# A two-block network on one core: the odd layer's last value units between its heads, maxima broadcast by DMA, low parts in halves, and gates evicted with their functions

## The reference

```
first_block:  proj = rmsnorm(x) @ w_in                     # 3592 columns
              h += [fox_attention(8 heads), hgrn(4 heads)] @ w_out
              h += memory_cross_attention(rmsnorm(h), rmsnorm(mem), w_q, w_kv, w_o)
              h += relu(rmsnorm(h) @ w1)^2 @ w2
second_block: cond = silu(c)
  layer 0:    x += g1 * pool_attention_mixer(modulate(rms_norm(x)))
              x += g2 * ((silu(h @ w1) * (h @ w3)) @ w2),  h = modulate(rms_norm(x))
  layer 1:    x += g1 * mlstm_mixer(modulate(rms_norm(x)))
              x += g2 * (the same gated FFN)
hgrn:         f = lb + (1 - lb) * sigmoid(gf); g = log f; k = 1 - f; q = silu(gq); i = gi
              S_t = diag(f_t) S_{t-1} + k_t i_t^T;  o_t = S_t^T q_t;  rmsnorm(o) * silu(gg)
mlstm:        z = h @ w_in                # q|k 1024, v 1024, o 1024, gates 32
              q, k = silu(conv5(z_qk)); per head and direction, with F = cumsum(log f):
              w[s,t] = exp(F_t - F_s + i_s - m_t), masked to one side
              y_t = sum_s (q_t.k_s / 8) w[s,t] v_s / max(|sum_s ...|, exp(-m_t))
              out = sigmoid(o) * head_gain * rms_norm(y_forward + y_backward) @ w_out
```

## Time and profile before

| | us |
|---|---|
| median of three runs | 2356.7 (2354.33 to 2357.33) |
| the profiled execution | 2348.1 |
| its span | 2346.0 |
| PE busy | 2171.9 (93%) |
| POOL busy | 818.5 (35%) |
| mean granted clock of PE | 0.948 |

### The profile page before, as it was taken

One profiled execution on the slowest core, in us unless ns is written; L12 is line 12 of the kernel. 1 busy time (PEld: TensorE's weight loads), 2 busy tenths in 40 slices (PEclk: granted clock), 3 DMA queues, 4 the chain that ended last, 5 costly groups with the idle time before them and its releaser, 6 DMA issues.

```text
span 2346.0 us, 26426 instructions
## 1 busy us (share of the span) xinstructions
PE 2171.9 (93%) x10170; PEld 1730.2 (74%) x10170; DVE 1121.2 (48%) x1852; ACT 710.1 (30%) x970; POOL 818.5 (35%) x295
## 2 busy tenths in 40 slices
PE   6998978898899999989988999999999878999998
PEld 5885367786778878876357888887798557888887
DVE  4112594453388886554536666722375554111112
ACT  3124533333332232333433212223233323222221
POOL 2441042461334334434013443333343332444342
PEclk8997878999899999988999999999999889999999
DMA  4230002241445553321014555532231002332322
GB/s 136 88 101 1 1 10 74 95 138 36 157 148 179 179 179 108 103 90 54 1 49 149 180 180 179 167 98 77 90 100 63 1 17 73 99 99 90 107 85 77
DMA packets 220417, 226.14 MB, mean 96 GB/s; under 512 B 3787, under 2 KB 218524, under 8 KB 220188
## 3 DMA queue, kind: packets, MB, share of 16 engines
q1 hardware_dynamic: 220316, 224.78, 29.5%
HBM read 222.67 MB, written 2.10 MB: 96 GB/s over the span
## 4 chain that ended last, share of the span: by engine, by line
PE 80%; DVE 8%; issue 7%; ACT 3%; POOL 1%; DMA 0%; DVEq 0%; SPq 0%; ACTq 0%; POOLq 0%
PE ps L1690 23%; PE ps L1692 23%; PE ps L1691 23%; PE ps L1821 2%; PE ps L1801 1%; DVE adacc L1368 1%; PE ps L1906 1%; PE ps L1843 1%; PE ps L1794 1%; PE ps L1757 1%; ACT wH L631 1%; PE ps L1812 1%; DVE T L1064 1%; DVE uL L1049 1%; DVE hnL L1051 0%
## 5 line engine op out<-in xcount | busy, mean ns | idle before, releaser
L511 POOL TENSOR_TENSOR wL<-raw,wH 128x2048 fp32r<-128x2048 f32 (+2 forms) x161 | 729.4, 4531 | 1274.3 <-ACT wH L631 1259.4
L1690 PE MATMUL ps<-hnH,wH 128*128 128x512 f32 x1336 | 530.8, 397 | 26.1 <-DVE hnL L1051 14.4
L1692 PE MATMUL ps<-hnH,wL 128*128 128x512 f32 x1336 | 526.1, 394 | 0.0
L1691 PE MATMUL ps<-hnL,wH 128*128 128x512 f32 x1336 | 525.5, 393 | 0.0
L631 ACT ACTIVATE wH<-raw 128x2048 fp32r<-128x2048 f32 (+2 forms) x161 | 302.4, 1879 | 648.8 <-PE ps L1692 624.8
L1690 PE MATMUL ps<-uH,wH 128*128 128x512 f32 x864 | 341.6, 395 | 10.5 <-DVE uL L1049 8.2
L1692 PE MATMUL ps<-uH,wL 128*128 128x512 f32 x864 | 338.6, 392 | 0.0
L1691 PE MATMUL ps<-uL,wH 128*128 128x512 f32 x864 | 338.5, 392 | 0.0
L1690 PEld LDWEIGHTS ps<-hnH,wH 128*128 128x128 f32 x1336 | 254.6, 191 | 80.7 <-issue 28.9
L1692 PEld LDWEIGHTS ps<-hnH,wL 128*128 128x128 f32 x1336 | 253.9, 190 | 54.0
L1691 PEld LDWEIGHTS ps<-hnL,wH 128*128 128x128 f32 x1336 | 254.6, 191 | 52.4 <-issue 0.5
(11 more groups left out here) (327 smaller groups left out, 2452.4 us busy)
## 6 DMA issues: line engine op xcount, KB each, us to landing
raw<-in_ffn_w_dram SPq DMA_DIRECT2D x60, 1024.0 KB, 5.3
adaw<-in_ada_w_dram SPq DMA_DIRECT2D x48, 1024.0 KB, 7.3
raw<-in_w_dram SPq DMA_DIRECT2D x32, 1024.0 KB, 5.3
raw<-in_w_in_dram SPq DMA_DIRECT2D x14, 1024.0 KB, 5.4
raw<-in_od_w_in_dram SPq DMA_DIRECT2D x12, 1024.0 KB, 5.3
raw<-in_w_xkv_dram SPq DMA_DIRECT2D x8, 1024.0 KB, 5.3
raw<-in_ffn_w_dram SPq DMA_DIRECT2D x8, 768.0 KB, 4.2
raw<-in_ev_w_in_dram SPq DMA_DIRECT2D x5, 1024.0 KB, 5.2
```

The source lines that it names most:

```text
L511: nc.gpsimd.tensor_tensor(wL[n % 2][:, 0:kc, 0:c], raw[n % 2][:, 0:kc, 0:c], wH[n % 2][:, 0:kc, 0:c].bitcast(F32), ALU.subtract).then_inc( ...
L1690: nc.tensor.matmul(out_ap, wh, xh, start=first, stop=False)
L1691: nc.tensor.matmul(out_ap, wh, xl, start=False, stop=False)
L1692: return nc.tensor.matmul(out_ap, wl, xh, start=False, stop=last)
```

## The change

1. `low` is made in two halves over k, so `w_lo` counts two for a unit (and SP's wait is for both). `unit_ready` waits for the first half, and a new `unit_whole` for the second, at the middle of a feature unit's first block; token units wait for both at once.
2. The gates' six units of the first stage are evicted by ACT straight from the banks with Silu or Sigmoid. The forget row's chain on ACT moves from unit 8 to unit 11, the four Ln come at unit 12, and DVE's gate steps stand ahead of the fox attention.
3. `norm_highs` makes the second unit's high after its third chunk. 
4. In `out`, ACT's squares of x are spread between other work, and xkv's second high stands ahead of the last two of them.
5. In the odd layer the output-gate units come first (units 5 to 8), one value unit is left ahead of the heads (unit 9), and three (10 to 12) run between the heads, in 18 portions of 5, 5 and 6 chunk steps (a step is 3 matmuls), three portions per head in heads 0 to 5, in banks 4 and 5. Their highs are made by ACT at odd heads, their lows by POOL at the end of heads 1, 3 and 5; `od_out`'s unit 0 is the last of these, and the high of its unit 1 is made at head 7 (hence `gated_norm` from 1), with its low on POOL behind the last head. DVE takes a block at the fifth tile of heads 1 to 6. The convolutions stand beside the takes of q and k and of the output gates. SP writes the maxima once to DRAM and reads each of the 16 rows back, broadcast over 128 partitions, into a ring of four SBUF tiles; L2122 is gone. The weights lie in four slots of four tiles, and the decayed scores are written over them; `ma` is gone. ACT's exps of slot s wait for `l_o` of slot s-4.

```diff
@@ -91,7 +91,7 @@
             add("od_w_in_2", 0, KC, 3104 - P, P, 1)
-            for c0 in range(D, 3 * D, UC):
+            for c0 in (*range(2 * D, 3 * D, UC), *range(D, 2 * D, UC)):
                 add("od_w_in_2", 0, KC, c0, UC)
@@ -111,9 +111,23 @@
-BY_ACT = [u[0].startswith("ffn_w1") for u in UNITS for _ in range(u[5])]
+GATE_UNITS = (7, 8, 9, 10, 13, 14)
+BY_ACT = [u[0].startswith("ffn_w1") or n in GATE_UNITS for n, u in enumerate(UNITS) for _ in range(u[5])]
 TAKEN = [sum(not x for x in BY_ACT[:b]) for b in range(len(BY_ACT) + 1)]
...
+V_FILL = (BLOCK0[AT["od_in"][0] + 10], BLOCK0[AT["od_in"][0] + 13])
+def bank(b):
+    return 4 + b % 2 if V_FILL[0] <= b < V_FILL[1] else b % 4
+def last_in_bank(b):
+    return b - 2 if V_FILL[0] + 2 <= b < V_FILL[1] else b - 4
@@ -312,9 +331,15 @@
     hgain = place("hgain", [P, D], F32, AR + 49408)[0]
-    wt = [place(f"wt{i}", [P, S], F32, ULOFF + 2048 * i)[0] for i in range(WT_RING)]
+    wt = []
+    for i in range(4):
+        offset = [ULOFF + 5120 * i] * TB
+        for j in range(1, TB):
+            offset[j] = offset[j - 1] + 512 * (TB - j + 1 if i % 2 == 0 else j)
+        if i == 3:
+            offset = [AR + 57088, ULOFF + 15360, AR + 55552, AR + 53504]
+        wt.append([place(f"wt{i}{j}", [P, (TB - j if i % 2 == 0 else j + 1) * P], F32, offset[j])[0] for j in range(TB)])
     cy = place("cy", [P, KC, S], F32, UHOFF)[0]
-    ma = [[place(f"ma{i}{d}", [P, TB, S], F32, HN + 8192 * (2 * i + d))[0] for d in range(2)] for i in range(2)]
     hsq = T
@@ -494,7 +522,21 @@
             sp.dma_start(hgain[:], a["od_head_gain_2"].rearrange("o h v -> o (h v)").to_broadcast([P, D])).then_inc(gain_in, 16)
-            loads(AT["od_in"][0] + 2, AT["ff2_1"][0])
+            n = AT["od_in"][0]
+            loads(n + 2, n + 12)
+            sp.wait_ge(r_rows, 2)
+            sp.dma_start(mrows, Mrow[:]).then_inc(mrow_out, 16)
+            sp.wait_ge(mrow_out, 16)
+            sp.wait_ge(r_tr, 2)
+            for s in range(2 * ML_H):
+                h, d = s // 2, s % 2
+                if s >= BC_RING:
+                    sp.wait_ge(l_w, 4 * (s - BC_RING) + 4)
+                row = h + 32 * d
+                sp.dma_start(bcr[s % BC_RING][:], mrows[row:row + 1, :].to_broadcast([P, S])).then_inc(bc_in[s % BC_RING], 16)
+                if s in (3, 7, 11, 15):
+                    load(n + 12 + s // 4)
+            loads(n + 16, AT["ff2_1"][0])
             gated_ffn(1)
@@ -508,8 +550,9 @@
                 pool.wait_ge(w_hi, (n if value is None else value) + 1)
-                nc.gpsimd.tensor_tensor(wL[n % 2][:, 0:kc, 0:c], raw[n % 2][:, 0:kc, 0:c],
-                                        wH[n % 2][:, 0:kc, 0:c].bitcast(F32), ALU.subtract).then_inc(w_lo, 1)
+                for k0, k1 in ((0, kc // 2), (kc // 2, kc)):
+                    nc.gpsimd.tensor_tensor(wL[n % 2][:, k0:k1, 0:c], raw[n % 2][:, k0:k1, 0:c],
+                                            wH[n % 2][:, k0:k1, 0:c].bitcast(F32), ALU.subtract).then_inc(w_lo, 1)
@@ -605,6 +648,8 @@
                     nc.gpsimd.tensor_tensor(hs[:, :, hv], hs[:, :, hv], mo[:, :, hv], ALU.mult).then_inc(n_g, 1)
+                if h in (1, 3, 5):
+                    low(n + 11 + h // 2)
             lows(AT["od_out"][0] + 1, AT["ff2_1"][0])
@@ -670,9 +715,11 @@
-            def norm_highs(q0, shift=None):
+            def norm_highs(q0, shift=None, unit=None):
                 for j in range(KC):
                     norm_high(q0, j, shift)
+                    if j == 2 and unit is not None:
+                        high(unit)
@@ -740,7 +777,17 @@
                 high(n + 1)
-                if u == 8:
+                if u in GATE_UNITS:
+                    dst, func = {7: (gq, ACT.Silu), 9: (gk, ACT.Sigmoid), 13: (gg, ACT.Silu)}[u - (u + 1) % 2]
+                    for c in range(2):
+                        b = BLOCK0[n] + c
+                        act.wait_ge(blk_done, b + 1)
+                        nc.scalar.activation(dst[:, 2 * ((u + 1) % 2) + c, :], ps[b % 4][:], func).then_inc(silu_done, 1)
+                if u == 12:
+                    for hh in range(HG_H):
+                        act.wait_ge(h_fk, hh + 1)
+                        nc.scalar.activation(lnf[:, hh, :], lnf[:, hh, :], ACT.Ln).then_inc(h_ln, 1)
+                if u == 11:
@@ -796,11 +843,14 @@
                     high_op(Q0["mem"] + j, memH[:, j, :], mT[j % 2][:], (m_t, j + 1))
-            squares("x", BLOCK0[n], range(KC))
+                squares("x", BLOCK0[n], range(2 * half, 2 * half + 2))
+            m = AT["xkv"][0]
+            squares("x", BLOCK0[n], range(4, 6))
+            high(m + 1)
+            squares("x", BLOCK0[n], range(6, KC))
             nc.scalar.activation(warm, eps, ACT.Sqrt)
...
             n = AT["xkv"][0]
-            high(n + 1)
             high(n + 2)
@@ -928,12 +976,17 @@
             def output_gate(u):
-                act.wait_ge(blk_taken, TAKEN[BLOCK0[n + 9 + u] + 2])
+                act.wait_ge(blk_taken, TAKEN[BLOCK0[n + 5 + u] + 2])
                 nc.scalar.activation(mo[:, :, u * UC:(u + 1) * UC], mo[:, :, u * UC:(u + 1) * UC], ACT.Sigmoid).then_inc(o_sig, 1)
-            for u in range(2, 8):
+            for u in range(2, 5):
                 high(n + u)
+            conv_silus(range(0, 2))
+            high(n + 5)
+            conv_silus(range(2, 3))
+            high(n + 6)
+            conv_silus(range(3, 4))
+            high(n + 7)
             act.wait_ge(r_sel, 1)
@@ -941,21 +994,16 @@
             nc.scalar.activation(erow[:], erow[:], ACT.Exp, scale=-1.0).then_inc(r_em, 1)
+            output_gate(0)
+            output_gate(1)
             high(n + 9)
-            conv_silus(range(0, 2))
+            output_gate(2)
+            conv_silus(range(4, 8))
             high(n + 10)
+            output_gate(3)
             act.wait_ge(r_tr, 2)
...
             nc.scalar.activation(ecol[:], ps[7][:, 0:256].rearrange("p (a b) -> p a b", a=TB), ACT.Copy).then_inc(r_cols, 1)
-            conv_silus(range(2, 5))
-            high(n + 11)
-            conv_silus(range(5, 8))
-            high(n + 12)
-            output_gate(0)
-            output_gate(1)
-            high(n + 13)
-            output_gate(2)
-            output_gate(3)
             act.wait_ge(r_cols, 2)
@@ -967,15 +1015,17 @@
             for h in range(ML_H):
+                if h % 2:
+                    high(n + 11 + h // 2)
                 for d in range(2):
+                    s = 2 * h + d
+                    act.wait_ge(bc_in[s % BC_RING], 16 * (s // BC_RING + 1))
+                    if s >= 4:
+                        act.wait_ge(l_o, s - 3)
                     for j in range(TB):
-                        r = 8 * h + 4 * d + j
                         lo, hi = (j * P, S) if d == 0 else (0, (j + 1) * P)
-                        act.wait_ge(l_bc, 2 * h + d + 1)
-                        if r >= WT_RING:
-                            act.wait_ge(l_a, r - WT_RING + 1)
                         row = h + 32 * d
-                        nc.scalar.activation(wt[r % WT_RING][:, lo:hi], ps[4 + d][:, lo:hi], ACT.Exp,
+                        nc.scalar.activation(wt[s % 4][j][:], bcr[s % BC_RING][:, lo:hi], ACT.Exp,
                                              bias=ccol[:, j, row:row + 1]).then_inc(l_w, 1)
@@ -1534,8 +1567,26 @@
+            def convolution(j):
+                for k in range(CONV_K):
+                    tap = cols[:, V_CW + 8 * k + j:V_CW + 8 * k + j + 1]
+                    src = cz[:, j, k:k + S]
+                    if k == 0:
+                        chain(nc.vector.tensor_scalar(cy[:, j, :], src, tap, cols[:, V_CB + j:V_CB + j + 1], ALU.mult, ALU.add))
+                    else:
+                        ins = nc.vector.scalar_tensor_tensor(out=cy[:, j, :], in0=src, scalar=tap, in1=cy[:, j, :],
+                                                             op0=ALU.mult, op1=ALU.add)
+                        if k < CONV_K - 1:
+                            chain(ins)
+                        else:
+                            ins.then_inc(c_y, 1)
...
                 take(b + j, cz[:, j, 2:2 + S], ps[(b + j) % 4][:])
+                if j >= 4:
+                    convolution(j - 4)
             gate_block = b + 8
@@ -1600,10 +1633,9 @@
                 dve.wait_ge(l_qk, 4 * h + j + 1)
-                if h >= 2:
-                    dve.wait_ge(l_o, 2 * h - 4 + d + 1)
-                nc.vector.scalar_tensor_tensor(out=ma[h % 2][d][:, j, lo:hi], in0=ps[j][:, lo:hi], scalar=FOX_D ** -0.5,
-                                               in1=wt[r % WT_RING][:, lo:hi], op0=ALU.mult, op1=ALU.mult).then_inc(l_a, 1)
+                w = wt[r // 4 % 4][j][:]
+                nc.vector.scalar_tensor_tensor(out=w, in0=ps[j][:, lo:hi], scalar=FOX_D ** -0.5, in1=w,
+                                               op0=ALU.mult, op1=ALU.mult).then_inc(l_a, 1)
@@ -1635,6 +1667,8 @@
                     decayed(8 * h + x)
```

(64 more changed lines are left out.)

113 lines of the change are left out of this document (47 added, 66 removed).

## The result

| | us |
|---|---|
| median before (4 runs) | 2355.5 |
| median of the changed kernel (4 runs) | 2322.65 (2316.3 to 2325.7) |
| ratio | 0.9872, 95% interval 0.9854 to 0.9889 |
| its profiled execution, span | 2325.7, 2324.0 |

Faster by 1.3%, 33 us; forecast were 57 us and 2300, with a range up to 2322, and 2322.65 lies just outside it. So the traces have 22 us to explain.

A forecast was written before the change was run, and what follows sets the result against it. PE, busy 93% of 2346.0 us, was taken as the bound. Terms -4.4 - 10 - 9 - 2 + 2 - 37 + 1.5 = -59, taken as -57: 2348.1 to 2291, plus 8.6 gives 2300 us; range 2284 to 2322.

The forecast's parts named there:

- Halved lows: Feature units start after half a low: first stage's unit 1, the unit after the narrow block, out's unit 1; -4.4 us.
- Gates: Gate functions and logarithms leave the fox attention for the first stage, removing PE's waits and half clock; -10 us (-16 to -7).
- xkv: Unit 1's high moved ahead of the last two squares, so PE starts at about 443 instead of 450.84; -9 us (-10 to -6).
- Conditioning: PE's products on adacc: DVE can get in between low halves at eight places; -2 us (-4 to 0).
- Norms: Five norms: low halves now fall on chunks 3 to 5; four places come out even, one loses 2.5; +2 us.
- rival C: Ports: DVE isn't let in between the halves, norms +12.8 and tail +5; 2314 us, chance 0.14.
- Odd layer: Three value units leave the stretch before the mLSTM heads and fill heads 0 to 5; together -37 us (-42 to -25).
- Heads 6 and 7: mLSTM heads without fills: chain loses broadcast matmul and exps' wait, 13.54 to about 11.5 us, -4, taken as -3.
- Tail: Behind the last head, od_out unit 1's low holds POOL while DVE's L1659 must start: +3.3, -1.7; +1.5 us (0 to +5).
- Rival B: In the mLSTM heads, fills lie in the PE-DVE-PE chain, +2.9 us a head, +17; 2317 us, chance 0.17.
- Rival E: Clock stays up nearly everywhere: -16 us in the fox attention, -42 in the heads; 2289 us, chance 0.05.
- Rival D: In the odd layer's heads each of 16 broadcasts is exposed, +66 us, net +9; 2366 us, chance 0.06.

The follow-up runs named there:

- e10: The changed kernel with the second part undone: gates taken by DVE, functions and logarithms within the fox attention as before; 2336.7 us, ratio to before 0.9921.
- e7: The changed kernel with each low made whole, in one instruction, so the first part undone; 2331.8 us, ratio to before 0.9913.
- e2: The changed kernel with DVE's sums of head h-3 at the start of head h instead of behind heads_out(h, 0); 2298.8 us, ratio to before 0.9773.
- e5: The changed kernel with the third part undone: the next unit's high ahead of the first chunk again in all five norms; 2307.8 us, ratio to before 0.9814.
- e6: The changed kernel with the low of od_out's unit 1 on POOL starting only after DVE has scaled all eight heads; 2312.6 us, ratio to before 0.9830.

## Why the forecast was too low, step by step

- **Halved lows, -4.4.** Measured -5.4 in the first stage and -0.9 in `out`, in the changed kernel's trace. Right in kind, 2 us better.
- **Gates, -10.** -8.3 in the trace, -14 by e10. Right. The longest wait for ACT left in the fox attention is 0.7 us.
- **xkv, -9.** -9.6. Right: the high stands at 422.99, and unit 1 starts at 428.24 without a wait.

```profile
422.99 1.90 ACT L676 ACTIVATE wH<-raw 128x2048 fp32r<-128x2048 f32 x1
...
428.24 0.28 PE L1725 MATMUL ps<-memH,wH 128*128 128x256 f32 x1
```

- **Conditioning, -2.** -1.2, at one place in `ff2_0`; in `ff1` nothing. The number is near, but the step was wrong. DVE does get in between the halves, and then the next `uL` meets the second half: two take 2.47 and 2.88 us, together 5.28, and before it was 5.29. PE still waits at eight places, 0.85 to 1.84 us (before 0.85 to 0.97). Nor is the 1.2 the halves': e7, with whole lows, has it too. Why that one wait is gone stays open; in e10 it stands, 1.26 us.

```profile
643.96 5.28 DVE L1430 TENSOR_TENSOR uL<-T,uH 128x512 fp32r<-128x512 f32 x2 [1.63 <-ACT uH L885]
```

- **Norms, +2.** +10: by place +1.8, +0.7, +3.6, +2.1 and +1.9. The mechanism was right (DVE does get in between the halves, 5.19 for two lows that take 4.67 alone, so rival C falls), its size was not. "The four places that were hit already come out even" took the 1.5 us that the first chunk wins as a gain of PE's; but two `hnL` are hit where it was one. In `ff2_0` PE starts on the first chunk 1.4 us earlier, but waits 1.21 us for the second of them and 1.84 instead of 0.97 at `adacc`, behind which the clock falls once more: from 1257.3 to 1260.7 PE ran at 0.5, and before's trace has no such fall.
- **Odd layer, -37.** -8.7. This is the step that failed. "From the end of `heads_out(h-1,1)` on, the square, the product and the low should be over after 6.7 us" left out the square's second wait. Head 1 has no such wait (`head_squares(0)` needs no sum), and there it held: a low at 1771.9, no wait at unit 11. In heads 3 and 5 the square came 9 us later. I had part of the evidence: in before's trace the same product starts 7.6 us behind its head's first `out_rows`, right ahead of the selects (the square ahead of it stands right behind a sum that ends at 1848.46), and "an estimated 1.1 us of slack" was counted from the operation's inputs, not from its row:

```profile
1849.26 1.27 POOL L607 TENSOR_TENSOR hs<-hs,mo 128x512 f32<-128x512 f32 x1 [9.14 <-ACT T L965]
1850.48 2.00 POOL L595 TENSOR_SCALAR_AFFINE_SELECT wt<-wt 128x128 f32<-128x128 f32 x8
```

- Its sum, from first scores to last `out_rows`, is 135.4 us where before took 106.9 and the forecast comes to 105.5; e2 took 109.5. Of the 26 us above e2 the wait at unit 12 with its half clock is 22.3 - 14.4 = 7.9, the late selects 17.9 - 11.1 = 6.8, the last period 14.3 - 9.6 = 4.7, and a fall of the clock in the first head 3.1; 3.4 lie in the last head. Of the 7.9, some 3 are a longer stay at half clock that not every trace has: it lasted 10.2 us here, and 3.4 us in e5, e6 and e10, whose odd layer is the same code and where this period is 19.3 to 19.4. The PE work per head was mis-sized too: 14.42 and not 13.8, 3 us in five periods. My rows gave 8.4 + 5.8 = 14.2; the 0.4 that I took off for a slow clock was not there.
- **Heads 6 and 7, -3.** 17.9 and 14.3 in the changed kernel, but 11.1 and 9.6 in e2, better than the 11.5 forecast. The chain was seen rightly, but it was held up by the same square, or e2 would not have shortened it.
- **Tail, +1.5.** +1.6, of +3.35 (9.80 for 6.45) and the wait at unit 1 gone. Right; e6 takes it back.

Rival B (fills in the chain) is not it: e2's five undisturbed periods are PE's own work. Rival E isn't: the clock is 0.78 and 0.86 in its two stretches. Rival D isn't either. The broadcasts (`mrows`, DMA issues as in rows 9) land in 5.0 and 3.8 us, and of ACT's idle time before the exps 24.7 us end by `out_rows` and nothing by a DMA (a group of lines: count, busy us, mean ns, idle time and what ended it):

```profile
R<-mrows SPq DMA_DIRECT2D x8, 256.0 KB, 5.0
sq<-mrows SPq DMA_DIRECT2D x8, 256.0 KB, 3.8
...
L1028 ACT ACTIVATE wt<-R,ccol 128x512 f32<-128x512 f32 (+3 forms) x32 | 15.2, 550 | 24.7 <-PE ps L2175 24.7
```

## What to carry to other kernels

Work that is put on a helper engine starts when the instruction ahead of it in that engine's order ends, so take its time from that instruction's row in the trace, with the releaser in the bracket, and follow the releaser back, a second wait (here a buffer of two freed by a sum) included. When one stage stops being the bound, ask of every instruction that was hidden in it where it stands and who frees it; one moved reduction was worth 24 us here, and 6 at most in the kernel before. And a move that helps the first chunk of a pipeline can harm the chunks on which PE is already working.
